# A second engine for the low half of the weights: GpSimd beside VectorE

## What is computed

```python
for l in range(DEPTH):
    u = rms_norm_2(h, norm_pre_mix[l])
    p = (u @ w_in[l]).astype(jnp.float32)
    ...
    mixed = jnp.concatenate([o_ret, o_hgrn, o_ml, o_rw], axis=-1).astype(h.dtype) @ w_out[l]
    h = h + rms_norm_2(mixed, norm_post_mix[l])
    u = rms_norm_2(h, norm_pre_ffn[l])
    ffn = (jax.nn.silu(u @ w_ffn_gate[l]) * (u @ w_ffn_up[l])) @ w_ffn_down[l]
    h = h + rms_norm_2(ffn, norm_post_ffn[l])
```

## Time and profile before

| what | value |
|---|---|
| median of 3 runs | 3925.11 us |
| lowest and highest of them | 3915.49 and 3926.25 us |
| the profiled execution, whole | 3918.05 us |
| its span, first to last instruction | 3916.7 us |
| mean granted TensorE clock | 0.984 of full speed |
| PE, DVE, ACT, POOL busy | 97%, 58%, 46%, 3% of the span |

### The profile page before, as it was taken

How to read it: one execution, slowest core, us unless ns; L and a number is a source line. 1 busy time by engine, 2 the same in 40 slices (tenths; PEclk the granted TensorE clock), 3 DMA queues, 4 the chain that set the end, 5 groups by cost and what they waited for, 6 DMA issues and landing times.

```text
span 3916.7 us, 49184 instructions
## 1 busy us (share of the span) xinstructions
PE 3797.8 (97%) x19948; PEld 3203.5 (82%) x19948; DVE 2255.0 (58%) x3526; ACT 1794.1 (46%) x2519; POOL 104.3 (3%) x61
## 2 busy tenths in 40 slices
PE   8999999999999999989999999999999989999998
PEld 7886778787898897778888888888988778888887
DVE  5665666675555746764454444566656664445444
ACT  6454545445454424444444444545325454444443
POOL 0000000000010000000000000010000000000000
PEclk9999999999999999999999999999999999999999
DMA  7655546563554405446666655544225446666654
GB/s 239 183 168 146 145 135 178 158 188 101 182 165 134 122 26 159 146 145 190 191 188 189 201 194 193 172 127 146 63 72 153 156 140 189 190 191 189 201 194 169
DMA packets 341427, 628.34 MB, mean 160 GB/s; under 512 B 21089, under 2 KB 63025, under 8 KB 340433
## 3 DMA queue, kind: packets, MB, share of 16 engines
q1 hardware_dynamic: 331920, 611.53, 51.4%
q10 hardware_dynamic: 9280, 13.69, 1.0%
HBM read 623.04 MB, written 2.10 MB: 160 GB/s over the span
## 4 chain that ended last, share of the span: by engine, by line
PE 88%; DVE 6%; ACT 3%; POOL 1%; issue 1%; DMA 1%; SPq 0%; ACTq 0%; DVEq 0%; POOLq 0%
PE bank L621 74%; DVE weights_low L527 2%; PE bank L745 2%; PE bank L1301 1%; PE bank L1398 1%; PE bank L2499 1%; PE bank L2513 1%; PE bank L2106 1%; PE bank L2512 1%; ACT weights_high L514 1%; PE bank L600 1%; PE bank L1381 1%; POOL stat L706 1%; PE bank L1304 0%; POOL arena L706 0%
## 5 line engine op out<-in xcount | busy, mean ns | idle before, releaser
L527 DVE TENSOR_TENSOR weights_low<-weights,weights_high 128x1024 fp32r<-128x1024 f32 (+3 forms) x1176 | 1393.8, 1195 | 980.6 <-ACT weights_high L514 969.1
L514 ACT ACTIVATE weights_high<-weights 128x1024 fp32r<-128x1024 f32 (+3 forms) x1176 | 1205.8, 1030 | 1345.2 <-PE bank L621 1289.6
L621 PE MATMUL bank<-weights_high,x_high 128*128 128x512 f32 (+3 forms) x2816 | 1117.1, 397 | 22.2 <-DVE weights_low L527 12.0
L621 PE MATMUL bank<-weights_low,x_high 128*128 128x512 f32 (+3 forms) x2816 | 1086.3, 386 | 0.0
L621 PE MATMUL bank<-weights_high,x_low 128*128 128x512 f32 (+3 forms) x2816 | 1085.9, 386 | 0.0
L621 PEld LDWEIGHTS bank<-weights_high,x_high 128*128 128x128 f32 x2816 | 535.8, 190 | 136.2 <-DVE weights_low L527 19.5
L621 PEld LDWEIGHTS bank<-weights_low,x_high 128*128 128x128 f32 x2816 | 534.7, 190 | 102.4
L621 PEld LDWEIGHTS bank<-weights_high,x_low 128*128 128x128 f32 x2816 | 536.3, 190 | 93.0
L621 PE MATMUL bank<-x_high,weights_high 128*128 128x256 f32 x960 | 279.6, 291 | 12.7 <-DVE arena L650 6.0
L621 PE MATMUL bank<-weights_high,ff_high 128*128 128x512 f32 x704 | 274.1, 389 | 0.0
L621 PE MATMUL bank<-weights_low,ff_high 128*128 128x512 f32 x704 | 273.9, 389 | 0.0
(11 more groups left out here) (381 smaller groups left out, 3613.4 us busy)
## 6 DMA issues: line engine op xcount, KB each, us to landing
weights<-in_w_in_dram SPq DMA_DIRECT2D x208, 512.0 KB, 3.6
weights<-in_w_ffn_gate_dram SPq DMA_DIRECT2D x176, 512.0 KB, 3.7
weights<-in_w_ffn_up_dram SPq DMA_DIRECT2D x176, 512.0 KB, 3.7
weights<-in_w_ffn_down_dram SPq DMA_DIRECT2D x176, 512.0 KB, 3.6
weights<-in_w_out_dram SPq DMA_DIRECT2D x128, 512.0 KB, 3.6
weights<-in_even_w_in_dram SPq DMA_DIRECT2D x88, 512.0 KB, 3.6
weights<-in_odd_w_in_dram SPq DMA_DIRECT2D x80, 512.0 KB, 3.7
weights<-in_mem_w_kv_dram SPq DMA_DIRECT2D x32, 512.0 KB, 4.0
```

Of the source, the lines that this page charges most:

```text
L514: self.high_mark[g] = self.high_split.count(act.ran(nc.scalar.activation(high, raw, ACT.Copy)), act.clock)
L527: self.low_mark[g] = self.low_split.count(dve.ran(nc.vector.tensor_tensor(low, raw, high.bitcast(F32), ALU.subtract)), dve.clock)
L621: ins = pe.ran(nc.tensor.matmul(out, l, r, start=(u + c + x + y == 0), stop=(u == blk.n - 1 and c == UNIT - 1 and y == 1)))
```

## The change

In `lows`, each subtraction is put on POOL in place of DVE if two things hold in the plan. With `begin` the planned time of the high half, POOL's end is planned at `max(pool.clock, begin) + 3.0`. This must be earlier than DVE's, `max(dve.clock, begin) + 1.2`, and earlier than `last`, the planned clock of PE plus 2.5 us for each unit between the one that PE is at and this one. POOL then waits for the high half, subtracts, and counts on a semaphore of its own, for which PE waits in `chunk_matmuls`. Nothing else is changed; the values are the same subtraction on another engine.

```diff
--- before.py
+++ after.py
@@ -330,6 +330,7 @@
             self.loaded = [Counter(sem(f"weights_loaded{i}"), 16) for i in range(RAW)]
             self.high_split = Counter(sem("high_split"))
             self.low_split = Counter(sem("low_split"))
+            self.low_split_pool = Counter(sem("low_split_pool"))
             self.unit_used = Counter(sem("unit_used"))
             self.bank_summed = Counter(sem("bank_summed"))
             self.first_loads = Counter(sem("ident_and_gains"), 16)
@@ -516,13 +517,20 @@
 
     def lows(self, least=-1):
 
-        nc, dve = self.nc, self.dve
+        nc, dve, pool = self.nc, self.dve, self.pool
         while self.no_low:
             g = self.no_low[0]
             if g > least and expected_at([self.high_mark[g]]) > max(dve.clock, self.pe.clock) + PATIENCE:
                 return
             w = self.units[g][0].width
             raw, high, low = self.raw[g % RAW][:, :, 0:w], self.w_high[g % HIGH][:, :, 0:w], self.w_low[g % RAW][:, :, 0:w]
+            begin, last = expected_at([self.high_mark[g]]), self.pe.clock + (g - self.g) * 2.5
+            if max(pool.clock, begin) + 3.0 < min(max(dve.clock, begin) + 1.2, last):
+                pool.wait_ge(self.high_mark[g])
+                self.low_mark[g] = self.low_split_pool.count(
+                    pool.ran(nc.gpsimd.tensor_tensor(low, raw, high.bitcast(F32), ALU.subtract)), pool.clock)
+                self.no_low.pop(0)
+                continue
             dve.wait_ge(self.high_mark[g])
             self.low_mark[g] = self.low_split.count(dve.ran(nc.vector.tensor_tensor(low, raw, high.bitcast(F32), ALU.subtract)), dve.clock)
             self.no_low.pop(0)
```

## The result

The changed kernel takes 3987.55 us (median of 4, 3984.38 to 3995.0) against 3920.47 for the kernel before in the same comparison: 1.0173 times as long, with a 95% interval of 1.0159 to 1.0186. That is 67 us slower, where 3920 was forecast and the range ended at 3938. Its profiled execution took 3989.26 us, with a span of 3987.6.

What follows compares the result with a forecast made beforehand. PE, busy 97% of the span, was taken as the bound, with gains possible only in mixed stages. Terms -11 + 10 + 1 + 0 = 0 us on 3918.05, set at 3920 toward the three-run median; range 3902 to 3938.

Steps and rivals of the forecast that it cites:

- How many move: Subtractions going from DVE to POOL, nearly all in mixed stages: about 100, with 60 to 150 as the ends.
- A subtraction on POOL: Duration of one weight subtraction on POOL: 1.9 us alone, taken from the nearest row, L2081.
- The gain: Relief of DVE: 20 chain subtractions fit the rule, 22.5 us; half counted, -11 us, ends 0 and -22.5.
- The holds: DVE held by POOL's SBUF reads: 21 chain instructions at 0.95 us, half covered, +10 us, ends 0 and +36.
- the cover by PE's stream: PE has matmuls to run meanwhile, so half of the 20 us of holds on the chain was not counted.
- The rival of shared reading: In norms and recurrences POOL comes first and DVE stands up to 1.7 us: about 3943 us, chance 0.2.
- Its point of decision: The shared-reading rival decides from 22.5 / 1.7 = 13 full holds on the chain, of the 21.
- POOL's queue: Moved subtractions delay POOL's later work, above all the power of L706: one delay, +1 us, ends 0 and +9.
- The plan: Changed planned clocks reorder the mixed stages: 0 us, ends -8 and +8, one stage-change place more or less.
- the first rival: POOL works in DVE's shadows and mixed stages get shorter: about 3898 to 3905 us, chance 0.24.
- its signs: Profile after: some 160 POOL instructions, DVE 120 us less busy, its subtractions longer than 1195 ns, PE's 22.2 us waits unchanged.
- Its sign of being wrong: Wrong if far over 150 move, POOL's take over 3 us alone, or PE's idleness changes over 10 us.

Runs made afterwards that it cites:

- e3: Changed kernel, all orders kept, each of the 111 POOL subtractions replaced by two memsets that read nothing from SBUF: 3883.44 us, ratio 0.9913.
- e1: Changed kernel's order on PE, ACT and SP and its planned clocks, but the 111 subtractions run on DVE: 3911.39 us, ratio 0.998.
- e10: Order of the kernel before, 102 mixed-stage subtractions moved to POOL where DVE is planned not to be late: 3920.32 us, ratio 0.9998.
- e13: e8 with all orders kept and two memsets in place of each subtraction on POOL: 3941.29 us, ratio 1.0051.
- e8: Changed kernel, but the plan charges DVE 1.2 us also for subtractions on POOL; the rule then picks 165: 4018.94 us, ratio 1.0254.
- e9: Order of the kernel before on PE, ACT and SP, 165 subtractions moved to POOL by the change's own rule: 3986.07 us, ratio 1.0175.

## Why the prediction was wrong, point by point

**How many move.** Right: 111, where about 100 were read from the lateness of DVE's subtractions in the trace.

**A subtraction on POOL.** Taken as 1.9 us from L2081 alone; measured 2.4 us undisturbed. POOL's groups:

```profile
L531 POOL TENSOR_TENSOR weights_low<-weights,weights_high 128x1024 fp32r<-128x1024 f32 x92 | 251.4, 2734 | 2073.0 <-ACT weights_high L515 2072.7
L2089 POOL TENSOR_TENSOR arena<-arena 128x1024 f32<-128x1024 f32 x14 | 28.9, 2071 | 82.2 <-DVE arena L2102 73.2 <-DVE arena L658 5.3 <-DVE arena L1906 3.7
```

The row chosen, L2081, has one of its inputs as one column repeated over the block; a subtraction of two whole tensors takes 2.4 us. Whether the repeated column makes the difference wasn't run. The mean is 2.7 because POOL is held too. The estimate from the Trainium skill ("GPSIMD Engine Reference", section 4.1), 2 x 1.23 = 2.5 us, was nearer than my row; the trace decides, at 2.4.

**The gain.** Half of 22.5 us was counted, 11; measured 28 us with nothing held (e3 against e1), 22 in the old order. The chain's pieces that fit the rule, 22.5 us, have about the size of the whole gain, so the half for PE's cover was the mistake. That the gain came at just these pieces wasn't traced. By the spans of e1 and e3, 3905.8 and 3881.6 us, 16 us of it is less idle time of PE and 5 us less loss to the clock.

**The holds.** This is the step that failed. Their existence, their length of up to 1.7 us, the kinds of instruction concerned and the rival's mechanism were read rightly: two SBUF inputs yes, PSUM no. The sum was not. It was 21 holds on the chain times 0.95 us times a half for PE's cover, 10 us. What the runs show is 71 holds of 126 us in all, 104 us of the kernel's time (the change against e3), and 0.75 to 0.86 us of it for each us held. Three parts of that sum were wrong. The first is the count, 71 in place of 21: only instructions on the chain of before were counted, as if the others had slack. The prediction itself had 52 of 101 moves meeting a two-input instruction, which was near: 68 of the 111 held one or two instructions. That the others had no slack because the rule picks stretches in which DVE is behind is argued; e10 shows only that few holds come where it isn't behind. The second is the mean: 0.95 us a hold against 126 / 71 = 1.8 us. The mean of a random meeting was the wrong one: 45 of the 71 were held for 1.9 us or more, nearly the whole of a subtraction on POOL. The third is the cover by PE's stream, taken as half: in the order of before that was about right (0.44 to 0.55 of each us held reached the end), in the order of after 0.75 to 0.86 reached it. Together, 71/21 x 1.8/0.95 x 0.86/0.5 is about 11, which takes the 10 us to some 110. The likely reason of the third, argued and not shown, is that the new plan counts VectorE 1.2 us freer for each move and so leaves PE less to do meanwhile.

**The balance.** The rival of shared reading was put at 3943 with a chance of 0.2, from 21 full holds of 1.7 us with half the gain. It named the right mechanism and direction; its time, too, is 45 us short of the 3988, by the same count of 21. Its point of decision, 13 full holds on the chain (22 us), was passed by far, with 104 us lost to holds.

**POOL's queue.** One power delayed was counted, 1 us. DVE's waits for the power of L1923 are 18.1 us, as before; right.

**The plan.** Put at 0 with ends of 8 us. The order alone is worth -7 us (e1), so right for this change. But e13 shows that an order can be 43 us worse than another with the same moves and no holds, so the ends were too near.

**The sums and the signs.** For the first rival the prediction gives 3898 to 3905, but its own terms, 3918 - 16 to 3918 - 26, make 3892 to 3902. Of its signs, the count on POOL and the longer mean of DVE's subtractions (1217 against 1195 ns) came; that DVE would be 120 us less busy and that PE's 22.2 us of waits for subtractions would stay did not (2258 against 2255 us; 50.4 us). Its sign of being wrong, over 10 us of change in PE's idleness, showed with 49.

## What the runs showed that was not expected

POOL can be shut out for long. A subtraction on POOL took 12.21 us, of 2.4 us of work:

```profile
884.71 12.21 POOL L531 TENSOR_TENSOR weights_low<-weights,weights_high 128x1024 fp32r<-128x1024 f32 x1 [7.28 <-ACT weights_high L515]
```

Beside it on DVE:

```profile
883.66 1.22 DVE L535 TENSOR_TENSOR weights_low<-weights,weights_high 128x1024 fp32r<-128x1024 f32 x1
884.80 1.29 DVE L1137 TENSOR_TENSOR arena<-arena 128x512 f32<-128x512 f32 x2
886.00 1.22 DVE L535 TENSOR_TENSOR weights_low<-weights,weights_high 128x1024 fp32r<-128x1024 f32 x1
887.14 1.28 DVE L1137 TENSOR_TENSOR arena<-arena,params 128x512 f32<-128x512 f32 x2
888.34 1.43 DVE L1137 TENSOR_TENSOR x_room<-arena,const 128x256 f32<-128x256 f32 x4
889.68 1.09 DVE L1137 TENSOR_TENSOR arena<-arena,const 128x256 f32<-128x256 f32 x3
890.69 1.22 DVE L535 TENSOR_TENSOR weights_low<-weights,weights_high 128x1024 fp32r<-128x1024 f32 x1
891.83 0.42 DVE L1137 TENSOR_TENSOR arena<-arena,const 128x256 f32<-128x256 f32 x1
892.16 0.75 DVE L1137 TENSOR_TENSOR arena<-arena,x_room 128x256 f32<-128x256 f32 x2
892.83 1.22 DVE L535 TENSOR_TENSOR weights_low<-weights,weights_high 128x1024 fp32r<-128x1024 f32 x1
893.97 0.75 DVE L1137 TENSOR_TENSOR arena<-arena,x_room 128x256 f32<-128x256 f32 x2
894.81 3.19 DVE L535 TENSOR_TENSOR weights_low<-weights,weights_high 128x1024 fp32r<-128x1024 f32 x1
```

DVE ran instructions with two SBUF inputs in an unbroken row, and POOL's end at 896.92 less its 2.4 us says that it came in only at about 894.6 us, where there is 0.1 us between two of them (893.97 + 0.75 = 894.72, and 894.81). Then DVE's next subtraction took 3.19 us in its turn, and PE stood:

```profile
896.97 0.79 PE L629 MATMUL bank<-weights_high,y_high 128*128 128x512 f32 x1 [5.34 <-POOL weights_low L531]
```

The Trainium skill ("SBUF — State Buffer", Who interferes with whom) tells that whichever starts first holds the shared pair for its instruction and that the other is blocked fully; the 2.65 us of L2613 and L2614 against 1.2 agree. Here the loser was passed over by 19 instructions in turn, from 884.80 to 894.72 us in the rows above. It is rare: the next longest of POOL's subtractions took 5.5 us, and the median is 2.4 us (ns):

```profile
L531 POOL TENSOR_TENSOR weights_low<-weights,weights_high x111: 1641/2405/12210, 31.1 to 3915.9; 128x1024 fp32r<-128x1024 f32 x92, 128x696 fp32r<-128x696 f32 x11, 128x688 fp32r<-128x688 f32 x4, 128x736 fp32r<-128x736 f32 x2
```

At 1131 us of the kernel before, POOL came in between two subtractions of DVE that also followed on each other without a gap. Why it did there and didn't at 884 us is open; no run was made on it.

The second surprise is the size of the clock's part. With the same work on PE, the loss to stretches with a granted clock of 0.50, its 1.2 GHz level, is 40 us in e3 and 84 in the changed kernel, so 44 of the 104 us that the holds cost come by way of the clock, after PE has stood still more often.

## What to carry to other kernels

Moving elementwise work from VectorE to GpSimd frees VectorE only as far as neither reads SBUF in the way of the other: here 111 moved subtractions left VectorE as busy as it was, and memsets in their place, which only write, held no two-input instruction. A planner that moves work to where it has room must ask whether both engines want the shared thing at that moment (a flat charge, as in e8, didn't help). A rule that picks the moments in which an engine is late picks those in which it is disturbed most often: 161 us of holds for 165 moves in e9, 19 us for 103 in e10. Asked also that no two-input instruction of VectorE be planned beside it, the same rule gave 0.37% less time than before (0.23 to 0.51) in place of 1.7% more; how much of this its new order gave is open.
